# Three edits in the second mixer of a transformer kernel: the query rotation on VectorE, attention steps inside weight chunks, output turns and splits moved

## The chip, the cores and the metric

The kernel runs on one core of a Trainium2 chip. The metric is the time of one launch on the device in microseconds (us), lower is better. TensorE multiplies, VectorE (DVE in the rows), ScalarE (ACT) and GpSimd (POOL) do the elementwise work, and SyncE (SP) issues the loads.

## The reference

The reference is a small network on 256 tokens of width 1024 in float32: a mixer of gated recurrence, a product-key feed-forward of 16384 experts, a second mixer of two kinds of attention, a second such feed-forward, and one more block. The change lies in the second mixer:

```python
def mla_moba_mixer(x, positions, norm_mix, w_in, cq_norm, ckv_norm, w_uq, w_ukv,
                   mla_q_norm, mla_k_norm, moba_q_norm, moba_k_norm, w_out):
    xn = rmsnorm(x, norm_mix)
    c_q, c_kv, k_pe, q_d, k_d, v_d = split_cols(xn @ w_in, [Q_LORA, KV_LORA, C_ROPE, D_W, D_W, D_W])
    q_c = (rmsnorm(c_q, cq_norm) @ w_uq).reshape(B, S, C_HEADS, C_QK)
    ...
    q_c = rmsnorm(q_c, mla_q_norm)
    q_c = jnp.concatenate([q_c[..., :C_NOPE], rope(q_c[..., C_NOPE:], positions)], axis=-1)
    ...
    return jnp.concatenate([out_c, out_d], axis=-1) @ w_out
```

Here `rope` rotates the last 64 of a head's 192 columns, as two halves of 32, with a sine and a cosine for each position. There are four heads of the first attention (numbers 0 to 3 below) and four of the second (4 to 7).

## The kernel before

**Weights.** All large weights pass through one stream of 680 chunks of 128x1024 numbers (512 KB) in four slots. For chunk `i`, SyncE loads `raw` once the low part of chunk `i-4` is made (`load`), ScalarE copies it to `WH`, rounded, once chunk `i-4` has been used (`high`), and VectorE or GpSimd subtracts, which gives the remainder `WL` (`low_v`, `low_g`). TensorE then makes each product three times: high by high, high by low and low by high (`three`). So an engine's program is a written order of such steps with the side work between them, and each engine goes through its own order strictly. A step that waits holds all that stands behind it on its engine.

**Second mixer.** It takes chunks `L1` to `L1+23`. Chunks 0 to 15 (`l1_win`) give `z = xn @ w_in` in four blocks of four chunks, and chunks 16 to 23 (`l1_wout`) the output projection. The remainders of chunks 0, 1 and 2 are GpSimd's, those of 3 to 23 VectorE's, and those of the first chunks of the feed-forward behind it GpSimd's again. Chunks 0 and 1 are multiplied token tile by token tile (`nat_by_tile`): tile 0 of both, the turn (transposes through TensorE) of the normed tile 1, and then tile 1 of both. After a block's last chunk ScalarE copies token tile 0 of its result from PSUM into `Z`, and VectorE token tile 1 (in chunks 3, 7, 11 and 15, once the chunk is used).

**Side work.** `side(c)` runs after chunk `c` on each engine. VectorE scales queries and keys in `side(9)`. GpSimd makes the eight small trigonometric tables `TRG` (line 1973), rotates the shared key part (lines 1982 to 1985, `KPE`) and rotates the queries (the same lines, 128x256 each time). TensorE turns queries and keys in `side(10)` and `side(11)` (`turn_heads`, line 1520; `qr` are the rotated query parts). Attention is a pipeline of ten steps, `att_tensor(0)` to `att_tensor(9)`: step `i` makes the scores of head `i` (line 1552), turns the weights of head `i-1` (line 1559) and weighs the values of head `i-2` (lines 1570 to 1572). `att_vector` and `att_scalar` of the same number follow it, and so does the copy of a head's output to `O`. Steps 0 to 3 stand after chunks 12 to 15, steps 4 to 9 among chunks 16 to 21. `turn_o(kp)` turns the outputs of heads `2kp` and `2kp+1` (line 1580), and `split_o_scalar` and `split_o_vector` (lines 1732 and 1736) make high and low parts of them for chunks `16+2kp` and `17+2kp`. `last_out` multiplies chunks 22 and 23.

**Loads for the tables.** SyncE issues, after the last low part of the feed-forward in front (`g_low`), eight small loads on one semaphore, `tables1_in`: row gains, constants, `UQ`, `UKV` and four columns `GCOL` (line 1508). The table makers wait for all eight, which is 128. Only then does SyncE go on with the weights from chunk `L1+4`.

Of the kernel before, what the change touches and what calls it, by code (L numbers as in the profile page):

```python
# [7 lines left out]
ALU = mybir.AluOpType  # L8
# [29 lines left out]
L0, P0, L1, P1, B2, END = 0, 32, 304, 328, 600, 680  # L38
# [37 lines left out]
def build(nc, d, out):  # L76
    ctx = ExitStack()
    with ctx:
# [3 lines left out]
        def sem(name):  # L82
            return ctx.enter_context(nc.semaphore(name))
# [121 lines left out]
                              [v[:, k, :] for v in rows], k == 0, k == nk - 1)  # L205
            m.then_inc(w_used, 1)

        def chunk_nat(t, i, outs, kq, n, bank_free):

            wait_low(t, i)  # L210
            for tt in range(2):
                if kq == 0:
                    bank_free(tt)
                for kk in range(2):
                    k = kq * 2 + kk
                    if n is not None:
                        rows_in(t, n, tt, k)
                    m = three(t, outs[tt], [v[:, k, tt * 128:tt * 128 + 128] for v in (XH, XL)],
                              [v[:, i % NW, kk * 512:kk * 512 + 512] for v in (WH, WL)], k == 0, k == 7)
            m.then_inc(w_used, 1)  # L220

        def nat_by_tile(t, i, n, xs):
# [13 lines left out]
                if tt == 0:  # L236
                    turn(t, n, 1, xs)

        def chunk_out(t, i, kp, nb, first, bank_free):

            wait_low(t, i)
            for tt in range(2):
                if first:
                    bank_free(2 * nb + tt)
                for kk in range(2):
                    k = 2 * kp + kk
                    m = three(t, PS[:, 2 * nb + tt, :], [v[:, k, tt * 128:tt * 128 + 128] for v in (XH, XL)],
                              [v[:, i % NW, kk * 512:kk * 512 + 512] for v in (WH, WL)], first and kk == 0, False)
            m.then_inc(w_used, 1)

        def last_out(t, i, kps, ready, n, xs):
# [1180 lines left out]

        def peer_gpsimd(g, l):
            wq, down, up = bases(l)
            for c in range(272):
                low_g(g, wq + c + 2)


        Z = ar(0, 2, 2048)
# [25 lines left out]
            "lora_products", "qkv_by_scalar", "qkv_by_vector"))  # L1465


        squares, hq_ss, hq_sd, scaled, rotated = (sem(n) for n in (
            "heads_squares", "heads_sum", "qk_root", "qk_scaled", "rotated"))
        mo_sd, mo_up, hT, hT_a, hT_v = (sem(n) for n in (  # L1470
            "moba_root", "moba_scaled", "heads_turned", "heads_by_scalar", "heads_by_vector"))
        at_mm, at_mx, at_e, at_T, pt_a, pt_v, at_w, o_a, o_v = (sem(n) for n in (
# [111 lines left out]
        def mixer1_tensor(t):  # L1584
            def nat_bank(nb, tt):
                if nb >= 2:
                    t.wait_ge(z_v if tt else z_a, nb - 1)

            def side(c):
# [35 lines left out]
                if c == 11:  # L1625
                    t.wait_ge(hT_a, 1)
                    t.wait_ge(hT_v, 1)
                    t.wait_ge(scaled, 3)
                    turn_heads(t, "kr")
                    t.wait_ge(hT_a, 2)  # L1630
                    t.wait_ge(hT_v, 2)
                    t.wait_ge(rotated, 2)
                    turn_heads(t, "qr")
                if c >= 12:
                    att_tensor(t, c - 12)
                if c == 13:
                    t.wait_ge(mo_up, 1)
                    t.wait_ge(z_a, 3)
# [9 lines left out]
            for c in range(2, 16):  # L1648
                nb, kq = divmod(c, 4)
                chunk_nat(t, L1 + c, [PS[:, 2 * (nb % 2) + tt, :] for tt in range(2)], kq, 2 if nb == 0 else None,  # L1650
                          lambda tt: nat_bank(nb, tt))
                side(c)
            turn_o(t, 0)
            att_tensor(t, 4)
            for n in range(6):
                kp, nb = divmod(n, 2)
                if nb == 0 and kp > 0:
                    turn_o(t, kp)
                if n in (2, 4):
                    att_tensor(t, 4 + n)  # L1660
                t.wait_ge(o_l, kp + 5)
                chunk_out(t, L1 + 16 + n, kp, nb, kp == 0,
                          lambda b: t.wait_ge(z_v if b % 2 else z_a, 3 + b // 2))
                if n == 0:
                    att_tensor(t, 5)
                if n in (2, 4):
                    att_tensor(t, 5 + n)
            turn_o(t, 3)
            last_out(t, L1 + 22, (3,), lambda kp: t.wait_ge(o_l, 8), 3, XS)


# [67 lines left out]
        def mixer1_scalar(a):  # L1739
# [69 lines left out]
            high(a, L1 + 19)  # L1809
            att_scalar(a, 5)  # L1810
            high(a, L1 + 20)
            high(a, L1 + 21)
            split_o_scalar(a, 1)
            att_scalar(a, 6)
            high(a, L1 + 22)
            att_scalar(a, 7)
            high(a, L1 + 23)
            split_o_scalar(a, 2)
            att_scalar(a, 8)
            high(a, L1 + 24)  # L1820
            att_scalar(a, 9)
            table(a, ACT.Sqrt)
            high(a, L1 + 25)
            split_o_scalar(a, 3)


        def by_head(ss, n):
# [47 lines left out]
        def mixer1_vector(v):  # L1875
            norm_vector(v, 2, XS, PV_MIX1, lambda t, h: add_up(v, 1, t, h, P0 + 271, 2), True)

            def side(c):
# [31 lines left out]
                if c == 9:  # L1910
                    v.wait_ge(hq_sd, 1)
                    v.reciprocal(SM[:, 64:80], SM[:, 64:80]).then_inc(vec.sem, vec.up())
                    v.wait_ge(vec.sem, vec.n)
                    v.tensor_tensor(kc4[:, :, :, 0:128], kv4[:, :, :, 0:128], by_head(SSQK[:, :, 1, :], 128),
                                    ALU.mult).then_inc(scaled, 1)
                    v.tensor_tensor(q8, q8, by_head(SSQK[:, :, 0, :], 192), ALU.mult).then_inc(scaled, 1)
                    v.wait_ge(rotated, 1)
                    v.tensor_tensor(kc4[:, :, :, 128:192], KPE.unsqueeze(2).to_broadcast([128, 2, 4, 64]),
                                    by_head(SSQK[:, :, 1, :], 64), ALU.mult).then_inc(scaled, 1)
                if c == 10:  # L1920
                    turned_vector(v, "kn")
                    turned_vector(v, "qn")
# [25 lines left out]
            low_v(v, L1 + 18)  # L1948
            att_vector(v, 5)
            low_v(v, L1 + 19)  # L1950
            low_v(v, L1 + 20)
            split_o_vector(v, 1)
            att_vector(v, 6)
            low_v(v, L1 + 21)
            att_vector(v, 7)
            low_v(v, L1 + 22)
            split_o_vector(v, 2)
            att_vector(v, 8)
            low_v(v, L1 + 23)
            att_vector(v, 9)  # L1960
            low_v(v, L1 + 24)
            split_o_vector(v, 3)
            low_v(v, L1 + 25)

        def mixer1_gpsimd(g):
            si, co = TRIG[:, 0], TRIG[:, 1]
            low_g(g, L1 + 2)
            g.wait_ge(trig_up, 2)
            g.wait_ge(tables1_in, 128)
            for n in range(2):  # L1970
                g1, g2 = (GN[:, 192 * n + lo:192 * n + lo + 32].unsqueeze(1).to_broadcast([128, 2, 32]) for lo in (128, 160))
                for i, (a_, b_) in enumerate(((co, g1), (si, g2), (co, g2), (si, g1))):
                    g.tensor_tensor(TRG[n][:, i], a_, b_, ALU.mult).then_inc(gps.sem, gps.up())

            def rotate(x1, x2, o1, o2, tables, shape, last):
                n = 64 * (shape[2] if len(shape) == 4 else 1)
                t1, t2, t3, t4 = (ROT[:, i * n:i * n + n].rearrange(
                    "p (t h c) -> p t h c" if len(shape) == 4 else "p (t c) -> p t c", t=2, c=32) for i in range(4))
                g.wait_ge(gps.sem, gps.n)
                for o, a_, b_ in ((t1, x1, 0), (t2, x2, 1), (t3, x2, 2), (t4, x1, 3)):  # L1980
                    b_ = tables[:, b_].unsqueeze(2).to_broadcast(shape) if len(shape) == 4 else tables[:, b_]
                    g.tensor_tensor(o, a_, b_, ALU.mult).then_inc(gps.sem, gps.up())
                g.wait_ge(gps.sem, gps.n)
                g.tensor_tensor(o1, t1, t2, ALU.subtract).then_inc(gps.sem, gps.up())
                g.tensor_tensor(o2, t3, t4, ALU.add).then_inc(last, 1)

            g.wait_ge(z_a, 1)
            g.wait_ge(z_v, 1)
            rotate(Z[:, :, 384:416], Z[:, :, 416:448], KPE[:, :, 0:32], KPE[:, :, 32:64], TRG[1], [128, 2, 32], rotated)
            for t in range(2):  # L1990
                g.wait_ge(qkv_a, 2 * t + 1)
                g.wait_ge(qkv_v, 2 * t + 1)
                g.tensor_tensor(SQS[:, t], QC[:, t], QC[:, t], ALU.mult).then_inc(squares, 1)
            g.wait_ge(scaled, 2)
            x1, x2 = q8[:, :, :, 128:160], q8[:, :, :, 160:192]
            rotate(x1, x2, x1, x2, TRG[0], [128, 2, 4, 32], rotated)
            g.wait_ge(hq_ss, 2)
            g.wait_ge(z_a, 3)
            g.wait_ge(z_v, 3)
            w = Z[:, :, 1024:1536]  # L2000
            g.tensor_tensor(SQS[:, :, 0:512], w, w, ALU.mult).then_inc(squares, 1)
            for c in range(1, 24):
                low_g(g, L1 + c + 2)
# [596 lines left out]
```

## Time and profile before

| | |
|---|---|
| median of three runs | 2155.51 us (2153.27 to 2156.95) |
| the profiled execution's own time | 2158.37 us |
| its span | 2156.4 us |
| TensorE busy | 2113.5 us (98%) |
| VectorE busy | 1466.3 us (68%) |
| ScalarE busy | 1279.6 us (59%) |
| GpSimd busy | 374.3 us (17%) |
| granted TensorE clock, mean | 0.997 of full speed |
| second mixer in the span | about 938 to 1053 us |

A profile is one execution. Times in the rows are from the start of its span. The ends of products on TensorE are modelled and overlap the next ones, so their starts are the firmer figure: a product with 512 columns starts every 0.23 us though its row says 0.39.

### The profile page before, as it was taken

Reading aid. Unit: us, or ns where it says so; the run is one execution under the profiler, and the core shown is the slowest. Engines: PE = TensorE matmul, PEld = TensorE weight load, DVE = VectorE, ACT = ScalarE, POOL = GpSimd, SP = SyncE. Lnnn points to the kernel's source line nnn. Section 1 sums busy time; section 2 is a strip of 40 time slices with the busy share of each in tenths; the row PEclk is TensorE's granted clock in tenths of the full one; section 3 lists DMA queues with packets and bytes.
Section 4 is the critical chain, followed back from the end, with each engine's and each line's share of the span. In section 5 each row is a group of like instructions: output and inputs, shape, how many; then the busy total and the mean of one; then the engine's idle time right before and its main releaser. Section 6 shows DMA issues by size and latency. Waiting matters only on the chain.

```text
span 2156.4 us, 32225 instructions
## 1 busy us (share of the span) xinstructions
PE 2113.5 (98%) x12416; PEld 1828.2 (85%) x12416; DVE 1466.3 (68%) x2588; ACT 1279.6 (59%) x2177; POOL 374.3 (17%) x175
## 2 busy tenths in 40 slices
PE   8899999999999999999999999999999999999998
PEld 7779988888888888877799888888888888788997
DVE  7658988889855555557489888898555555433446
ACT  6665488877644444455545888776444444444464
POOL 1437800000000000031378000000000000253131
PEclk9999999999999999999999999999999999999999
DMA  6445655555566666653456555555666666754244
GB/s 221 141 143 164 183 174 167 165 176 166 160 203 194 195 195 194 193 183 111 122 164 185 172 166 170 172 170 158 205 194 194 194 193 193 262 182 156 79 137 127
DMA packets 105179, 373.16 MB, mean 173 GB/s; under 512 B 12172, under 2 KB 15652, under 8 KB 104644
## 3 DMA queue, kind: packets, MB, share of 16 engines
q1 hardware_dynamic: 105028, 371.11, 56.4%
q8 instruction: 99, 1.62, 0.3%
q14 instruction: 52, 0.43, 0.1%
HBM read 369.97 MB, written 1.10 MB: 172 GB/s over the span
## 4 chain that ended last, share of the span: by engine, by line
PE 91%; DVE 4%; ACT 3%; issue 1%; DMA 1%; POOL 1%; SPq 0%; DVEq 0%; ACTq 0%; POOLq 0%
PE ps L186 22%; PE ps L180 17%; PE ps L182 16%; PE ps L181 16%; PE ps L187 11%; PE ps L1008 3%; PE ps L2100 1%; PE ps L2078 1%; DVE WL L168 1%; PE ps L987 1%; DMA raw<-in_w_qk_dram 1%; PE ps L2086 1%; PE ps L1552 0%; ACT arena L287 0%; ACT WH L163 0%
## 5 line engine op out<-in xcount | busy, mean ns | idle before, releaser
L163 ACT ACTIVATE WH<-raw 128x1024 fp32r<-128x1024 f32 x680 | 717.1, 1056 | 466.4 <-PE ps L182 406.9
L186 PE MATMUL ps<-X,WH 128*128 128x512 f32 x2048 | 727.2, 399 | 0.7 <-DVE WL L168 0.6
L168 DVE TENSOR_TENSOR WL<-raw,WH 128x1024 fp32r<-128x1024 f32 x552 | 676.2, 1227 | 72.2 <-ACT WH L163 72.0
L173 POOL TENSOR_TENSOR WL<-raw,WH 128x1024 fp32r<-128x1024 f32 x128 | 321.1, 2513 | 1663.1 <-ACT WH L163 1662.3
L187 PE MATMUL ps<-X,WL 128*128 128x256 f32 x2048 | 571.3, 279 | 0.0
L186 PEld LDWEIGHTS ps<-X,WH 128*128 128x128 f32 x2048 | 384.4, 188 | 89.4 <-DVE WL L168 1.0
L180 PE MATMUL ps<-WH,X 128*128 128x512 f32 x960 | 379.2, 395 | 7.6 <-DVE X L1736 3.4
L187 PEld LDWEIGHTS ps<-X,WL 128*128 128x128 f32 x2048 | 386.0, 188 | 0.1
L182 PE MATMUL ps<-WH,X 128*128 128x512 f32 x960 | 374.9, 390 | 0.0
L181 PE MATMUL ps<-WL,X 128*128 128x512 f32 x960 | 374.9, 390 | 0.0
L180 PEld LDWEIGHTS ps<-WH,X 128*128 128x128 f32 x960 | 181.0, 188 | 49.0 <-DVE X L1736 4.1
L182 PEld LDWEIGHTS ps<-WH,X 128*128 128x128 f32 x960 | 180.9, 188 | 38.2
L181 PEld LDWEIGHTS ps<-WL,X 128*128 128x128 f32 x960 | 181.1, 189 | 37.0 <-issue 0.5
L180 PE MATMUL ps<-X,WH 128*128 128x256 f32 x704 | 201.4, 286 | 0.7 <-DVE WL L168 0.7
L181 PE MATMUL ps<-X,WH 128*128 128x256 f32 x704 | 199.2, 283 | 0.0
L182 PE MATMUL ps<-X,WL 128*128 128x256 f32 x704 | 199.2, 283 | 0.0
L1385 DVE TENSOR_TENSOR X<-arena,X 128x512 fp32r<-128x512 f32 x84 | 58.1, 692 | 161.9 <-ACT X L1172 161.9
L1125 ACT ACTIVATE ONE<-ONE,GATE 128x128 f16<-128x128 f16 x512 | 167.4, 429 | 0.0
L180 PE MATMUL ps<-WH,GH 128*128 128x512 f32 x352 | 137.3, 390 | 2.7 <-DVE GL L1385 2.7
L180 PEld LDWEIGHTS ps<-X,WH 128*128 128x128 f32 x704 | 134.9, 192 | 5.6 <-issue 2.7
L182 PE MATMUL ps<-WH,GL 128*128 128x512 f32 x352 | 137.0, 389 | 0.0
L181 PE MATMUL ps<-WL,GH 128*128 128x512 f32 x352 | 137.0, 389 | 0.0
(306 smaller groups left out, 2375.9 us busy)
## 6 DMA issues: line engine op xcount, KB each, us to landing
raw<-in_l_down_dram SPq DMA_DIRECT2D x256, 512.0 KB, 3.7
raw<-in_l_up_dram SPq DMA_DIRECT2D x256, 512.0 KB, 4.2
raw<-in_l_wq_dram SPq DMA_DIRECT2D x32, 512.0 KB, 3.6
raw<-in_w_qk_dram SPq DMA_DIRECT2D x24, 512.0 KB, 3.8
raw<-in_w_gates_dram SPq DMA_DIRECT2D x24, 512.0 KB, 3.6
raw<-in_l_nat_dram SPq DMA_DIRECT2D x16, 512.0 KB, 3.5
raw<-in_l_wout_dram SPq DMA_DIRECT2D x16, 512.0 KB, 3.7
raw<-in_l_win_dram SPq DMA_DIRECT2D x16, 512.0 KB, 3.7
```

Of the source, the lines that this page charges most:

```text
L163: a.activation(WH[:, i % NW, :], raw[:, i % NW, :], ACT.Copy).then_inc(w_high, 1)
L168: v.tensor_tensor(WL[:, i % NW, :], raw[:, i % NW, :], WH[:, i % NW, :], ALU.subtract).then_inc(w_low_v, 1)
L173: g.tensor_tensor(WL[:, i % NW, :], raw[:, i % NW, :], WH[:, i % NW, :], ALU.subtract).then_inc(w_low_g, 1)
L180: t.matmul(o, a[0], b[0], start=first, stop=False)
L181: t.matmul(o, a[0], b[1], start=False, stop=False)
L182: return t.matmul(o, a[1], b[0], start=False, stop=last)
L186: t.matmul(PS[:, bank, :], w[0], X2[:, k, :, :].rearrange("p w t -> p (w t)"), start=first, stop=False)
L187: return t.matmul(PS[:, bank, 0:256], w[1], X2[:, k, 0, :], start=False, stop=last)
L987: m = t.matmul(PS[:, 4 + h % 4, (2 * tt + q) * 128:(2 * tt + q) * 128 + 128], QT[:, j, tt * 128:tt * 128 + 128], KEYS[:, j * 128:j * 128 + ...
L1008: m = t.matmul(PS[:, 6 + j // 4, (j % 4) * 128:(j % 4) * 128 + 128], ONE[:, s % 2, 0, g, :, tt], ROWS[:, s % 2, 1 + k, g, :, tt], start=(k ...
L1125: a.activation(ROWS[:, s % 2, 1, g, :, t], ROWS[:, s % 2, 2, g, :, t], ACT.Copy, scale=GATE0[:, 8 * s + j:8 * s + j + 1]).then_inc(row_0, 1)
L1385: v.tensor_tensor(gl, G[:, 2 * p:2 * p + 2, :].rearrange("p e t -> p (e t)"), gh, ALU.subtract).then_inc(g_low, 1)
```

## The change

GpSimd makes the tables first of all, before the remainders of chunks 0, 1 and 2, the first two of which move there from the end of the feed-forward's loop. VectorE rotates the queries in `side(9)`. Steps 1 to 3 of the attention on TensorE move from behind chunks 13 to 15 to inside them: after three, two and one of the chunk's four groups of three products. `turn_o(1)` to `turn_o(3)` move from behind chunks 17, 19 and 21 to the middle of them. ScalarE and VectorE split these outputs ahead of the weight copies that stood in front. Of the order on VectorE and ScalarE in chunks 13 to 15 nothing is changed.

```diff
-        def chunk_nat(t, i, outs, kq, n, bank_free):
+        def chunk_nat(t, i, outs, kq, n, bank_free, amid={}):
...
+                    if 2 * tt + kk + 1 in amid:
+                        amid[2 * tt + kk + 1]()
...
-        def chunk_out(t, i, kp, nb, first, bank_free):
+        def chunk_out(t, i, kp, nb, first, bank_free, amid=None):
...
+                if tt == 0 and amid:
+                    amid()
...
         def peer_gpsimd(g, l):
             wq, down, up = bases(l)
-            for c in range(272):
+            for c in range(270 if l == 0 else 272):
                 low_g(g, wq + c + 2)
...
-                    t.wait_ge(rotated, 2)
+                    t.wait_ge(rotated, 3)
                     turn_heads(t, "qr")
-                if c >= 12:
-                    att_tensor(t, c - 12)
+                if c == 12:
+                    att_tensor(t, 0)
...
                 chunk_nat(t, L1 + c, [PS[:, 2 * (nb % 2) + tt, :] for tt in range(2)], kq, 2 if nb == 0 else None,
-                          lambda tt: nat_bank(nb, tt))
+                          lambda tt: nat_bank(nb, tt), {16 - c: lambda: att_tensor(t, c - 12)} if c >= 13 else {})
                 side(c)
             turn_o(t, 0)
             att_tensor(t, 4)
             for n in range(6):
                 kp, nb = divmod(n, 2)
-                if nb == 0 and kp > 0:
-                    turn_o(t, kp)
-                if n in (2, 4):
-                    att_tensor(t, 4 + n)
                 t.wait_ge(o_l, kp + 5)
                 chunk_out(t, L1 + 16 + n, kp, nb, kp == 0,
-                          lambda b: t.wait_ge(z_v if b % 2 else z_a, 3 + b // 2))
-                if n == 0:
-                    att_tensor(t, 5)
-                if n in (2, 4):
-                    att_tensor(t, 5 + n)
-            turn_o(t, 3)
+                          lambda b: t.wait_ge(z_v if b % 2 else z_a, 3 + b // 2),
+                          (lambda: turn_o(t, kp + 1)) if nb else None)
+                if n < 5:
+                    att_tensor(t, n + 5)
             last_out(t, L1 + 22, (3,), lambda kp: t.wait_ge(o_l, 8), 3, XS)
...
             high(a, L1 + 20)
+            split_o_scalar(a, 1)
             high(a, L1 + 21)
-            split_o_scalar(a, 1)
             att_scalar(a, 6)
             high(a, L1 + 22)
             att_scalar(a, 7)
+            split_o_scalar(a, 2)
             high(a, L1 + 23)
-            split_o_scalar(a, 2)
             att_scalar(a, 8)
             high(a, L1 + 24)
             att_scalar(a, 9)
+            split_o_scalar(a, 3)
             table(a, ACT.Sqrt)
             high(a, L1 + 25)
-            split_o_scalar(a, 3)
...
+                    x1, x2 = q8[:, :, :, 128:160], q8[:, :, :, 160:192]
...
+                    v.wait_ge(tables_up, 8)
+                    v.wait_ge(scaled, 2)
+                    for o, x, i in ((t1, x1, 0), (t2, x2, 1), (t3, x2, 2), (t4, x1, 3)):
+                        v.tensor_tensor(o, x, TRG[0][:, i].unsqueeze(2).to_broadcast([128, 2, 4, 32]),
+                                        ALU.mult).then_inc(vec.sem, vec.up())
+                    v.wait_ge(vec.sem, vec.n)
+                    v.tensor_tensor(x1, t1, t2, ALU.subtract).then_inc(rotated, 1)
+                    v.tensor_tensor(x2, t3, t4, ALU.add).then_inc(rotated, 1)
...
         def mixer1_gpsimd(g):
             si, co = TRIG[:, 0], TRIG[:, 1]
-            low_g(g, L1 + 2)
             g.wait_ge(trig_up, 2)
             g.wait_ge(tables1_in, 128)
             for n in range(2):
...
-                    g.tensor_tensor(TRG[n][:, i], a_, b_, ALU.mult).then_inc(gps.sem, gps.up())
...
+                    g.tensor_tensor(TRG[n][:, i], a_, b_, ALU.mult).then_inc(tables_up, 1)
+            for c in range(3):
+                low_g(g, L1 + c)
...
-            g.wait_ge(scaled, 2)
-            x1, x2 = q8[:, :, :, 128:160], q8[:, :, :, 160:192]
-            rotate(x1, x2, x1, x2, TRG[0], [128, 2, 4, 32], rotated)
```

`split_o_vector(v, 1)`, `(v, 2)` and `(v, 3)` move on VectorE in the same way: the first ahead of `low_v(L1+20)`, the second ahead of `low_v(L1+22)`, the third stays behind `att_vector(v, 9)`. The calls `low_v(L1+24)` and `low_v(L1+25)`, which did nothing because these remainders are GpSimd's, are gone.

## Rows read from the trace of the kernel before

**Rows 1.** The page: the chain of work that ended last, by engine.

```profile
PE 91%; DVE 4%; ACT 3%; issue 1%; DMA 1%; POOL 1%; SPq 0%; DVEq 0%; ACTq 0%; POOLq 0%
```

**Rows 2.** TensorE's waits over the whole span: releaser, us in total, times, longest.

```profile
PE ps L180 <- DVE X L1736: 3.4, 3, 2.0
PE ps L1580 <- ACT arena L1727: 2.1, 1, 2.1
```

**Rows 3.** GpSimd's timeline, 934 to 951 us: start, us, engine, line, form, idle before.

```profile
934.47 4.75 POOL L173 TENSOR_TENSOR WL<-raw,WH 128x1024 fp32r<-128x1024 f32 x2 [666.99 <-ACT WH L163]
942.18 2.37 POOL L173 TENSOR_TENSOR WL<-raw,WH 128x1024 fp32r<-128x1024 f32 x1 [2.97 <-ACT WH L163]
944.51 5.27 POOL L1973 TENSOR_TENSOR arena<-trig,arena 128x64 f32<-128x64 f32 x8
```

**Rows 4.** The tile GCOL: its four loads, durations and starts, and time to landing.

```profile
L1508 SPq DMA_DIRECT2D gcol<-in_rows_dram x4: 427/479/542, 933.0 to 934.6; - x4
...
DMA to landing us min/median/max: 4.4/4.7/5.1
```

**Rows 5.** Line 1973, the tables: ns shortest, median and longest of eight.

```profile
L1973 POOL TENSOR_TENSOR arena<-trig,arena x8: 322/332/1313, 944.5 to 948.5; 128x64 f32<-128x64 f32 x8
```

**Rows 6.** TensorE's and VectorE's timelines at the mixer's start.

```profile
938.17 0.39 PE L180 MATMUL ps<-WH,X 128*128 128x512 f32 x1
...
942.20 1.09 PE L397 MATMUL ps<-cst,arena 128*128 128x128 f32 x8 [1.15 <-DVE arena L344]
943.74 0.50 PE L180 MATMUL ps<-WH,X 128*128 128x512 f32 x1 [0.45 <-DVE X L350]
...
945.84 3.76 DVE L168 TENSOR_TENSOR WL<-raw,WH 128x1024 fp32r<-128x1024 f32 x3 [0.34 <-ACT WH L163]
```

**Rows 7.** VectorE's timeline, 981 to 985 us.

```profile
981.62 0.68 DVE L1918 TENSOR_TENSOR arena<-arena,sm 128x512 f32<-128x512 f32 x1
982.22 1.75 DVE L168 TENSOR_TENSOR WL<-raw,WH 128x1024 fp32r<-128x1024 f32 x1
983.89 1.40 DVE L1690 TENSOR_SCALAR arena<-ps,gcol 128x512 f32<-128x512 f32 x2
```

**Rows 8.** TensorE's timeline: the turn of the rotated queries, and chunk 12.

```profile
988.64 1.03 PE L1520 MATMUL ps<-cst,arena 128*64 128x128 f32 x8 [1.89 <-POOL arena L1985]
989.43 0.48 PE L180 MATMUL ps<-WH,X 128*128 128x512 f32 x1
```

**Rows 9.** VectorE's, ScalarE's and TensorE's timelines behind chunk 15.

```profile
1009.98 0.69 DVE L1944 COPY arena<-ps 128x512 f32<-128x512 f32 x1 [0.58 <-PE ps L182]
1011.87 0.56 DVE L1852 SCALAR_TENSOR_TENSOR arena<-ps,arena 128x384 f32<-128x384 f32 x1 [1.20 <-PE ps L1552]
...
1013.11 0.40 ACT L1712 ACTIVATE arena<-arena,sm 128x128 f32<-128x128 f32 x1 [2.53 <-DVE sm L1856]
...
1015.13 0.63 PE L1580 MATMUL ps<-cst,arena 128*128 128x128 f32 x4 [2.15 <-ACT arena L1727]
```

**Rows 10.** ScalarE's and TensorE's timelines among chunks 17 to 22.

```profile
1023.37 0.61 ACT L1727 ACTIVATE arena<-ps,sm 128x128 f32<-128x128 f32 x2
...
1024.41 0.60 PE L1580 MATMUL ps<-cst,arena 128*128 128x128 f32 x4
...
1027.14 0.50 PE L180 MATMUL ps<-WH,X 128*128 128x512 f32 x1 [0.47 <-DVE X L1736]
...
1045.89 0.50 PE L180 MATMUL ps<-WH,X 128*128 128x512 f32 x1 [1.98 <-DVE X L1736]
```

**Rows 11.** Windows: TensorE busy, weight loads, DVE, ACT, POOL, granted clock, DMA share, GB/s.

```profile
84.00:87.00 3.00, 0.00 (x0) 0.00 (x0) 1.99 (x2) 2.98 (x3) 3.00 (x2) 1.00 0.49 175
88.00:91.00 3.00, 3.00 (x12) 2.52 (x12) 1.82 (x2) 1.04 (x2) 1.72 (x1) 0.53 0.26 96
...
1047.40:1050.70 3.30, 3.30 (x9) 2.58 (x8) 1.15 (x2) 0.72 (x2) 0.00 (x0) 0.50 0.56 159
```

More of the change, by code:

```diff
@@ L1465, in build @@
             "lora_products", "qkv_by_scalar", "qkv_by_vector"))
-        squares, hq_ss, hq_sd, scaled, rotated = (sem(n) for n in (
-            "heads_squares", "heads_sum", "qk_root", "qk_scaled", "rotated"))
+        squares, hq_ss, hq_sd, scaled, rotated, tables_up = (sem(n) for n in (
+            "heads_squares", "heads_sum", "qk_root", "qk_scaled", "rotated", "trig_gained"))
         mo_sd, mo_up, hT, hT_a, hT_v = (sem(n) for n in (
@@ L1919, in side @@
                                     by_head(SSQK[:, :, 1, :], 64), ALU.mult).then_inc(scaled, 1)
+                    x1, x2 = q8[:, :, :, 128:160], q8[:, :, :, 160:192]
+                    t1, t2, t3, t4 = (ROT[:, i * 256:i * 256 + 256].rearrange("p (t h c) -> p t h c", t=2, c=32)
+                                      for i in range(4))
+                    v.wait_ge(tables_up, 8)
[6 more added lines that the diff above has]
+                    v.tensor_tensor(x2, t3, t4, ALU.add).then_inc(rotated, 1)
                 if c == 10:
@@ L1950, in mixer1_vector @@
             low_v(v, L1 + 19)
+            split_o_vector(v, 1)
             low_v(v, L1 + 20)
-            split_o_vector(v, 1)
             att_vector(v, 6)
@@ L1955, in mixer1_vector @@
             att_vector(v, 7)
+            split_o_vector(v, 2)
             low_v(v, L1 + 22)
-            split_o_vector(v, 2)
             att_vector(v, 8)
@@ L1960, in mixer1_vector @@
             att_vector(v, 9)
-            low_v(v, L1 + 24)
             split_o_vector(v, 3)
-            low_v(v, L1 + 25)
         def mixer1_gpsimd(g):
             si, co = TRIG[:, 0], TRIG[:, 1]
-            low_g(g, L1 + 2)
             g.wait_ge(trig_up, 2)
@@ L1972, in mixer1_gpsimd @@
                 for i, (a_, b_) in enumerate(((co, g1), (si, g2), (co, g2), (si, g1))):
-                    g.tensor_tensor(TRG[n][:, i], a_, b_, ALU.mult).then_inc(gps.sem, gps.up())
[L1975 to L1985, printed above, removed]
+                    g.tensor_tensor(TRG[n][:, i], a_, b_, ALU.mult).then_inc(tables_up, 1)
+            for c in range(3):
+                low_g(g, L1 + c)
+            x1, x2, o1, o2 = Z[:, :, 384:416], Z[:, :, 416:448], KPE[:, :, 0:32], KPE[:, :, 32:64]
+            t1, t2, t3, t4 = (ROT[:, i * 64:i * 64 + 64].rearrange("p (t c) -> p t c", t=2) for i in range(4))
+            g.wait_ge(tables_up, 8)
             g.wait_ge(z_a, 1)
             g.wait_ge(z_v, 1)
-            rotate(Z[:, :, 384:416], Z[:, :, 416:448], KPE[:, :, 0:32], KPE[:, :, 32:64], TRG[1], [128, 2, 32], rotated)
+            for o, x, i in ((t1, x1, 0), (t2, x2, 1), (t3, x2, 2), (t4, x1, 3)):
+                g.tensor_tensor(o, x, TRG[1][:, i], ALU.mult).then_inc(gps.sem, gps.up())
+            g.wait_ge(gps.sem, gps.n)
+            g.tensor_tensor(o1, t1, t2, ALU.subtract).then_inc(gps.sem, gps.up())
+            g.tensor_tensor(o2, t3, t4, ALU.add).then_inc(rotated, 1)
             for t in range(2):
```

## The prediction, made before the change was run

> **What bounds the kernel now.** I read the page first. The chain that ended last is TensorE's for 91% of the span [rows 1], so only what moves TensorE's products counts, and all that lies behind the second mixer shifts with them. Then I read TensorE's own waits, because a stall of the bounding engine is the only thing that such a change can remove. In this mixer they are few: 2.1 us before the first turn of outputs and 3.4 us in three waits for split outputs [rows 2], and 1.9 us before the turn of the rotated queries [rows 8]. The last of the three costs more than it shows, for behind it the clock fell [rows 11]. Third came the timelines of all engines around every moved step. The reader should see there who is in front of the step on its own engine.
>
> **The tables go first: a loss at the start.** GpSimd now makes eight tables before the remainder of chunk 0, and they wait for eight loads. The last of these is issued at 934.6 and lands no earlier than 4.4 us later, at 939.0 (5.1 us: 939.7) [rows 4]. Before, GpSimd had chunk 0's remainder under way at 934.47 [rows 3], and TensorE's first products of the mixer stood at 938.17 [rows 6].
>
> How long do the tables take? They took 5.27 us [rows 3], yet the shortest of them 0.322, the median 0.332 and the longest 1.313 [rows 5]. The long ones lie where VectorE makes three remainders, 945.84 to 949.6 [rows 6]. In the new place VectorE makes none, for its first remainder comes after tile 1's rows. I take 8 x 0.33 = 2.6 us; the bound is 5.3. The Trainium skill's GPSIMD Engine Reference (Specifications) says that GpSimd shares its SBUF interfaces with VectorE and contends with its instructions of two SBUF inputs. The trace agrees (0.33 beside 1.31), and by that rule the sum has the short price.
>
> So tables end at 941.7. A remainder takes 4.75/2 = 2.37 us [rows 3], so those of chunks 0, 1 and 2 end at 944.0, 946.4 and 948.8. Chunk 0's six products on tile 0 start at 944.1, and chunk 1's at 946.5. Twelve products took from 938.17 to the last start at 942.20 - 1.15 - 0.39 = 940.66, so 0.227 us each [rows 6], and six take 1.4: 947.9. From the turn to tile 1's first product are 943.74 - 942.20 = 1.54 us [rows 6]. Tile 1 starts at 949.4 in place of 943.74: **5.7 us late at full clock.** TensorE idles from 938.2 to 944.1, 5.9 us. After an idle stretch that holds 84 to 87 us the granted clock was 0.53 in 88 to 91 [rows 11], so I expect half speed here. At 0.45 us each chunk 1's six products take 2.7, and tile 1 starts at 950.7: 7.0 us late. I take **+6.5**, ends +5.7 and +9.3 (tables at 5.3 us). Nothing absorbs it: loads of chunks 4 to 6 are issued behind these remainders, but chunk 4 is needed 8 us after tile 1 starts and a load takes some 4, and its two copies 2.3.
>
> **Queries rotated by VectorE.** The rotation's six operations are 128x256. VectorE shows 128x512 at 982.22 - 981.62 = 0.60 us from start to start [rows 7]. I take 0.33 (bounds 0.30, by elements alone, and 0.60), so with the wait between the four and the two 2.1 us (1.8 to 3.6), and nothing else hides it. Behind it on VectorE stand chunk 12's remainder (982.22 before, now 984.3; 1.2 us, a third of 3.76 [rows 6]) and the two copies of 0.7 us that took place at 983.89 [rows 7]. They end at 986.8, where TensorE's turn of the rotated queries needs them. That turn could start at 986.9 or after the turn in front of it: chunk 11 ends at 988.64 - 1.89 - 1.03 = 985.7 [rows 8], the turn of the rotated keys must wait for the first copy until 986.2 and takes 0.8. So chunk 12 starts at 987.8 and not at 989.43 [rows 8]: **-1.6**. No later weight is then late; VectorE has over 1 us of slack before chunks 13 and 14.
>
> **Steps 1 to 3 inside chunks 13 to 15: what VectorE does first decides.** TensorE does the same work in another order. Before, chunk 15 ended at 1009.8 and step 3 at 1012.8; now both are done at 1011.2, with the 1.6 us. The aim would be that step 3's chain runs under the chunk's last nine products. But in VectorE's order the copy of `Z` stands ahead of `att_vector(3)`, and it waits until chunk 15 is used. So the chain starts only at the chunk's end: 0.2 us to the copy and 0.6 for it, then 1013.11 - 1011.87 = 1.24 to ScalarE's exponentials, then 1015.13 - 1013.11 = 2.02 to the turn [rows 9]. 1011.2 + 4.1 = 1015.3, against 1015.13. **+0.1, and the 1.6 us before it are given back: +1.7.** TensorE idles 4.1 us there instead of 2.15. Near enough to the idle stretch in [rows 11] that I expect half clock behind it: 3.3 us at 0.50 lose 1.65, **+1.6** (0 if not).
>
> **Turns in mid-chunk, splits ahead of copies.** `turn_o(1)` needs head 3's output, whose copies end at 1023.98, and TensorE turns it at 1024.41 [rows 10]. In the middle of chunk 17, six products earlier, at 1023.0, it must wait till 1024.1. Then come the turn, six products (1.4) and step 6, which with the turn take 1027.14 - 0.5 - 0.2 - 1024.41 = 2.0: chunk 18 starts at 1027.5, against 1027.14 [rows 10]. The wait of 0.5 is gone and one of 1.1 is there. The same holds for `turn_o(2)`, where one of about 1.0 goes; both together cost 0.3. `turn_o(3)` is different: its head 7 is ready in time, half a chunk covers the splits of 0.6 and 0.7 us, and ScalarE's table load and chunk copy no longer stand ahead. The wait of 1.98 [rows 10] goes with 0.2 around it. Together **-1.9** (-1.4 to -2.0).
>
> **The clock behind `last_out`.** Behind that wait the clock was 0.50 for 1047.40 to 1050.70 [rows 11]; without the wait I expect full clock, **-1.6** (0 if it falls anyway). The Trainium skill's TensorE: Matmul & The Clock Gate (What's actually happening) says that the slow clock is the default and activity lifts it. By that rule, with which the trace agrees, the first two idle stretches cost and this one is won.
>
> **Sum.** +6.5 - 1.6 + 1.7 + 1.6 - 1.9 - 1.6 = +4.7 us on the profiled execution's 2158.4 (span 2156.4 and 2 us around it): 2163.1. The median of the runs is 2155.5, 2.9 below, so the forecast is 2155.5 + 4.7 = **2160.2 us**.
>
> **Rivals.**
> - *The clock does not fall* behind the two new idle stretches. For it: how long a fall lasts and when it begins is seen in two places only. Then 5.7 + 0.1 - 1.9 - 1.6 = +2.3: 2157.8 us.
> - *Step 3 does run under chunk 15.* VectorE's order speaks against it. The turn would come at 1011.5, 3.6 us early, without idling: 6.5 - 3.6 - 1.9 - 1.6 = -0.6: 2154.9 us.
> - *The other side, faster:* the table loads don't hold chunk 0. It decides whether all eight have landed by 934.47 - 2.6 = 931.9, or the tables are otherwise hidden. Then 0.1 - 1.9 - 1.6 = -3.4: 2152.1, and a little more with a better clock. Against it: the last load is issued at 934.6.
> - *Everything at its upper end:* tables at 5.3 us, half clock at all three places: 9.3 + 0.1 + 1.6 - 1.4 = +9.6: 2165.1 us.
>
> **How the numbers follow.** A measurement of this kernel tells about 0.2% (4.3 us) from no change. Chances: forecast 0.46 and upper end 0.08, both slower: 0.54. Clock rival 0.28 and step 3 rival 0.08: within 0.2%: 0.36. The other side 0.10, which I count as faster. The range goes from 2156.5, a little under the clock rival for the spread of medians, to 2165.0; it leaves out the step 3 rival and the faster one, 0.18.
>
> **What would show it.** On GpSimd the eight tables at 939 to 941.7 and then three remainders up to 948.8; TensorE's first product of the mixer at 944 and a wait for line 173, which the trace before hardly has; tile 1 near 950. Chunk 12 then starts 1.6 us earlier in relation to tile 1. VectorE's copy of line 1944 (its line after) ahead of step 3 with TensorE waiting 4 us before the first turn. Waits of about 1 us inside chunks 17 and 19, none before `last_out`. Granted clock of about 0.5 at the mixer's start and behind the first turn, 1.00 in `last_out`. I would be wrong if the tables start before 939, if the rotation on VectorE costs over 3 us, or if the clock stays up.

## The result, and the profile after

The changed kernel is slower: median 2164.33 us (2161.41 to 2165.19, six runs) against 2156.23 us (2153.27 to 2158.36, six runs) before. The ratio is 1.0037, with an interval of 1.0026 to 1.0048, or +8.1 us: small, but clear of the noise. The profiled execution took 2164.03 us (span 2162.1). The forecast was +4.7 us.

This page's chain by engine answers to [rows 1]: TensorE is still what sets the end.

```profile
PE 92%; DVE 3%; ACT 2%; issue 1%; POOL 1%; DMA 0%; SPq 0%; DVEq 0%; ACTq 0%; POOLq 0%
```

TensorE's waits, as [rows 2] (releaser, us in total, times, longest). The three waits for split outputs are gone. There is a new one of 7.5 us for GpSimd, and that for ScalarE grew from 2.1 to 3.9, with two more behind it:

```profile
PE ps L180 <- POOL WL L173: 7.5, 1, 7.5
PE ps L1585 <- ACT arena L1726: 5.7, 3, 3.9
```

The mixer's start, on SyncE, GpSimd and TensorE (start, us, engine, line, form, idle before and its releaser); these answer to [rows 3, 4, 6]:

```profile
928.55 2.46 SPq L1510 DMA_DIRECT2D arena<-in_l_uq_dram  x1
```

```profile
L1513 SPq DMA_DIRECT2D gcol<-in_rows_dram x4: 428/431/878, 931.5 to 933.4; - x4
...
DMA to landing us min/median/max: 3.9/4.6/4.8
```

```profile
938.35 2.71 POOL L1981 TENSOR_TENSOR arena<-trig,arena 128x64 f32<-128x64 f32 x8 [670.82 <-DMA gcol<-in_rows_dram]
941.01 7.00 POOL L173 TENSOR_TENSOR WL<-raw,WH 128x1024 fp32r<-128x1024 f32 x3
```

```profile
932.09 1.09 PE L402 MATMUL ps<-cst,arena 128*128 128x128 f32 x8 [0.19 <-DVE arena L349]
943.41 0.79 PE L180 MATMUL ps<-WH,X 128*128 128x512 f32 x1 [7.48 <-POOL WL L173]
...
950.30 0.50 PE L180 MATMUL ps<-WH,X 128*128 128x512 f32 x1 [0.45 <-DVE X L355]
```

This profile reached the mixer 2.4 us sooner than that of before (932.09 for the turn of tile 0 against 934.48), in code that nothing changed. The lead grows evenly through the first feed-forward. It isn't laid to the change: of two profiles of one and the same kernel, that with the short idle products below, one has it (931.52) and one hasn't (934.41). So each stage is measured from a mark inside the mixer. Three intervals carry the reading: from the turn of tile 0 to tile 1's first product (the start), from there to `turn_o(0)`, and from the turn of tile 0 to the first product of line 186 in the feed-forward behind the mixer (the stage).

| us | start | to `turn_o(0)` | stage |
|---|---|---|---|
| before | 9.26 | 71.39 | 130.69 |
| after | 18.21 | 71.74 | 138.43 |

The stage is 7.7 us longer, nearly the loss by the medians (8.1). The two profiled executions differ by 5.7, since one came to the stage sooner. The start alone lost 8.95; all behind it together won 1.2.

VectorE's timeline and TensorE's, as [rows 7, 8]: six rotations, then the remainder, and TensorE turns keys and queries in one go, with no wait for GpSimd.

```profile
988.76 1.42 DVE L1926 TENSOR_TENSOR arena<-arena 128x256 f32<-128x256 f32 x4
990.22 0.43 DVE L1929 TENSOR_TENSOR arena<-arena 128x256 f32<-128x256 f32 x1
990.56 0.42 DVE L1930 TENSOR_TENSOR arena<-arena 128x256 f32<-128x256 f32 x1
990.90 1.22 DVE L168 TENSOR_TENSOR WL<-raw,WH 128x1024 fp32r<-128x1024 f32 x1
```

```profile
992.88 1.91 PE L1525 MATMUL ps<-cst,arena 128*64 128x128 f32 x16 [0.46 <-issue]
994.54 0.47 PE L180 MATMUL ps<-WH,X 128*128 128x512 f32 x1
```

VectorE, ScalarE and TensorE behind chunk 15, as [rows 9]. The copy of `Z` still stands ahead of step 3, and TensorE, which was done with step 3 long before, waits 3.89 us:

```profile
1018.18 0.69 DVE L1955 COPY arena<-ps 128x512 f32<-128x512 f32 x1 [3.93 <-PE ps L182]
1018.79 0.55 DVE L1851 SCALAR_TENSOR_TENSOR arena<-ps,arena 128x384 f32<-128x384 f32 x1
```

```profile
1020.02 0.40 ACT L1711 ACTIVATE arena<-arena,sm 128x128 f32<-128x128 f32 x1 [1.24 <-DVE sm L1855]
```

```profile
1022.04 1.08 PE L1585 MATMUL ps<-cst,arena 128*128 128x128 f32 x4 [3.89 <-ACT arena L1726]
...
1033.60 0.63 PE L1585 MATMUL ps<-cst,arena 128*128 128x128 f32 x4 [0.92 <-ACT arena L1726]
...
1043.98 0.63 PE L1585 MATMUL ps<-cst,arena 128*128 128x128 f32 x4 [0.91 <-ACT arena L1726]
...
1053.63 0.50 PE L180 MATMUL ps<-WH,X 128*128 128x512 f32 x1
```

The lower three answer to [rows 10]: two waits of 0.9 inside chunks 17 and 19, and none before `last_out`.

Windows, columns as in [rows 11], with the window's length as the first figure; the granted clock comes before the DMA share. In the upper two it is half speed, each behind a long wait. In `last_out`, where before showed 0.50, it is 1.00:

```profile
940.00:948.00 8.00, 4.59 (x11) 3.60 (x12) 0.00 (x0) 0.00 (x0) 8.00 (x7) 0.50 0.35 105
...
1022.00:1026.00 4.00, 3.96 (x18) 3.70 (x18) 2.18 (x5) 0.92 (x3) 0.00 (x0) 0.50 0.01 4
...
1053.00:1057.00 4.00, 3.97 (x18) 2.96 (x17) 1.57 (x3) 3.03 (x5) 1.97 (x2) 1.00 0.40 131
```

### The profile page after: what moved, and what is told of

Read it like the earlier page. It is cut to its first block, busy times and chain, and to the rows that moved or that the text cites. A ratio compares the mean times of both kernels' runs of the same rounds, so it can differ in the third digit from the quotient of the medians.

```text
span 2162.1 us, 32225 instructions
## 1 busy us (share of the span) xinstructions
PE 2114.4 (98%) x12416; PEld 1831.3 (85%) x12416; DVE 1467.4 (68%) x2594; ACT 1280.2 (59%) x2177; POOL 364.9 (17%) x169
## 4 chain that ended last, share of the span: by engine, by line
PE 92%; DVE 3%; ACT 2%; issue 1%; POOL 1%; DMA 0%; SPq 0%; DVEq 0%; ACTq 0%; POOLq 0%
PE ps L186 22%; PE ps L180 17%; PE ps L182 17%; PE ps L181 17%; PE ps L187 11%; PE ps L1013 3%; PE ps L2102 1%; PE ps L2080 1%; DVE WL L168 1%; PE ps L992 1%; PE ps L1557 1%; PE ps L2088 1%; ACT arena L292 0%; DVE X L355 0%; PE ps L1035 0%
```

## The experiments

All medians stand beside that of before on the same chip. "Stage" and "start" are the intervals of the table above, in the one profile of each kernel. A profile that holds one more stretch of slow clock than another is some 1.7 us longer for it (`last_out` took 7.65 us with one and 6.02 without), so small differences between stages are no firmer than those between medians.

| kernel | median | before | ratio, interval | start | to `turn_o(0)` | stage |
|---|---|---|---|---|---|---|
| remainders first | 2154.69 | 2156.31 | 0.9994, 0.9985 to 1.0003 | 9.25 | 71.77 | 128.55 |
| + step 3 ahead of `Z` | 2149.62 | 2156.31 | 0.9969, 0.9958 to 0.9979 | 9.25 | 69.55 | 125.69 |
| + turns behind 17, 19 | 2150.31 | 2156.88 | 0.9965, 0.9951 to 0.9979 | 9.25 | 67.90 | 122.80 |
| tables first alone | 2164.24 | 2156.31 | 1.0038, 1.0024 to 1.0052 | 16.46 | 71.40 | 137.09 |
| turns and splits alone | 2155.38 | 2156.31 | 0.9993, 0.9984 to 1.0002 | 9.27 | 71.41 | 129.20 |
| rotation alone | 2154.02 | 2155.23 | 0.9991, 0.9982 to 0.9999 | 9.26 | 69.94 | 128.33 |
| steps inside alone | 2157.89 | 2155.23 | 1.0011, 1.0002 to 1.0019 | 9.26 | 73.14 | 131.68 |
| gains on their own semaphore | 2157.06 | 2155.23 | 1.0003, 0.9994 to 1.0012 | 10.90 | 71.75 | 131.32 |
| clock held, long | 2168.37 | 2155.23 | 1.0053, 1.0040 to 1.0066 | 21.31 | 74.41 | 141.63 |
| clock held, short | 2164.91 | 2156.88 | 1.0042, 1.0029 to 1.0056 | 16.06 | 71.77 | 133.74 |
| clock held, short, again | 2162.45 | 2154.82 | 1.0035, 1.0024 to 1.0046 | 15.90 | 71.74 | 133.61 |
| the change again | 2162.86 | 2154.82 | 1.0038, 1.0024 to 1.0052 | 17.33 | 71.74 | 137.55 |

**Undoing one part: the remainders of chunks 0 to 2 stand ahead of the tables again.**

```diff
         def mixer1_gpsimd(g):
             si, co = TRIG[:, 0], TRIG[:, 1]
+            for c in range(3):
+                low_g(g, L1 + c)
             g.wait_ge(trig_up, 2)
...
-            for c in range(3):
-                low_g(g, L1 + c)
```

> The changed kernel, but GpSimd makes the remainders of chunks 0, 1 and 2 before the tables, as before the change. Theory (the tables' loads hold the first chunk): in the changed trace the mixer's tile 1 stood 9.0 us late, so this kernel is 7 to 9 us faster than the changed one, 2155.5 to 2157.5 us, level with the kernel before within 2 us; TensorE's wait of 7.5 us for line 173 is gone and the granted clock stays at 1.00 at the mixer's start, while the wait of 3.9 us before the first turn and the clock of 0.5 behind it remain. Rival (the loss lies in the steps inside chunks): the time stays within 2 us of 2164, and the stall moves behind chunk 2.

Measured: 2154.69 us, 9.6 less than the whole change. The start is 9.25, as before. On GpSimd:

```profile
935.73 4.74 POOL L173 TENSOR_TENSOR WL<-raw,WH 128x1024 fp32r<-128x1024 f32 x2 [667.33 <-ACT WH L163]
...
945.77 5.26 POOL L1983 TENSOR_TENSOR arena<-trig,arena 128x64 f32<-128x64 f32 x8
```

The tables take 5.26 us here, beside VectorE's remainders, and 2.71 in the changed kernel's place, where VectorE had only two short operations. In this place nothing waits for them: the short tables were bought with TensorE's idling. The order on GpSimd, together with the wait for the loads that stands in it, is the loss.

**The other half of step 3: on VectorE and ScalarE it goes ahead of chunk 15's `Z` copy too** (on top of the last kernel; ScalarE in the same way).

```diff
             for c in range(16):
                 low_v(v, L1 + c + 2)
+                if c == 15:
+                    att_vector(v, 3)
                 if c % 4 == 3:
...
-                if c >= 12:
+                if 12 <= c < 15:
                     att_vector(v, c - 12)
```

> As e1_remainders_first, and in chunk 15 VectorE and ScalarE do step 3 of the attention ahead of their copies of Z. Theory (the copy of Z, which waits for the whole chunk, gives back what steps inside chunks gain): the wait before the first turn falls from 3.9 us to under 0.6 us, the clock stays at 1.00 behind it, and the time falls by 3.6 us for the chain and 2.5 us for the clock against e1, to about 2150 us, faster than the kernel before by 0.25%. Rival (the chain from scores to the output is the limit anyway): under 1 us of gain.

Measured: 2149.62 us, faster than before by 0.31%. VectorE's and TensorE's timelines:

```profile
1009.86 0.56 DVE L1853 SCALAR_TENSOR_TENSOR arena<-ps,arena 128x384 f32<-128x384 f32 x1 [0.70 <-PE ps L1557]
...
1013.09 0.69 DVE L1959 COPY arena<-ps 128x512 f32<-128x512 f32 x1 [1.96 <-PE ps L182]
```

```profile
1013.12 0.63 PE L1585 MATMUL ps<-cst,arena 128*128 128x128 f32 x4
```

Step 3 runs under the chunk's last products, and the first turn follows them with no wait. The stage is only 2.9 us shorter than the last kernel's: this profile, the slowest of its eight executions (2152.79), has slow clock at 943 to 948 (0.66) and at 1053 to 1057 (0.57), where the other has none. It was VectorE's and ScalarE's order that kept TensorE's new place for the step from being worth anything.

**The tables first, alone, on the kernel before.**

```diff
-            for c in range(272):
+            for c in range(270 if l == 0 else 272):
...
         def mixer1_gpsimd(g):
             si, co = TRIG[:, 0], TRIG[:, 1]
-            low_g(g, L1 + 2)
             g.wait_ge(trig_up, 2)
...
+            for c in range(3):
+                low_g(g, L1 + c)
```

> The kernel before with one edit: GpSimd makes the tables before the remainders of chunks 0, 1 and 2. Theory: the same loss as in the changed kernel, tile 1 of the mixer 7 to 9 us late with half clock for chunk 1's products, 2163 to 2165 us. Rival: the loss needs the other edits; then under 2 us.

Measured: +7.9 us, as much as the whole change, and TensorE's wait is there:

```profile
PE ps L180 <- POOL WL L173: 7.0, 1, 7.0
```

**The turns and splits alone** (`turn_o(1)` to `turn_o(3)` in mid-chunk, splits ahead of the weight copies; on the kernel before).

> The kernel before with only the outputs' turns in mid-chunk and the splits ahead of the weight copies. Theory: the waits of 0.5, 1.0 and 2.0 us before chunks 18, 20 and 22 become two of about 1 us inside chunks 17 and 19, which gives 1.7 to 1.9 us, and the clock stays up in the last chunks, which gives 1.6 us: 2152.7 us, 0.15% faster than before. Rival: the gain is lost inside the chunks, and the time is that of before within 1 us.

Measured: -0.9 us, not -2.8; the stage is 1.5 shorter. The waits are as forecast (0.92 and 0.91 inside, none before `last_out`), and the clock did stay up at 1047 to 1051. But it fell behind the wait of 2.15 us before the first turn, which is in the kernel before as well [rows 9] and had no fall behind it there (1.00 at 1015 to 1022):

```profile
1016.00:1020.00 4.00, 4.00 (x19) 3.63 (x18) 2.54 (x7) 1.53 (x6) 0.00 (x0) 0.57 0.01 4
...
1047.00:1051.00 4.00, 4.00 (x19) 3.30 (x18) 1.57 (x4) 2.58 (x6) 2.40 (x1) 1.00 0.44 131
```

So the waits' own time is won (3.43 us of them became 1.83), and the slow clock was as long in this profile as before. That the fall moved because a wait was removed isn't shown: the next kernel removes neither wait and shows the same.

**The rotation alone** (on VectorE, the rest as in the kernel before).

> The kernel before with only the rotation of the queries on VectorE (tables made behind the three remainders, attention steps, turns and splits as before). Theory: chunk 12 starts 1.4 to 1.6 us earlier, and as step 3 stands behind chunk 15 and the copy of Z is not in its way, all of it reaches the end: about 1.5 us faster than before, 2154.7 us. Rival: the rotation on VectorE (2.1 us) delays copies and remainders so much that nothing is gained.

Measured: -1.2 us by the medians, and the way from tile 1 to `turn_o(0)` is 1.45 shorter. TensorE's waits of 2.15 us before `turn_o(0)` (1013.86) and of 1.98 us before `last_out` (1046.10) are both there, as before. The windows behind them:

```profile
1013.00:1017.00 4.00, 3.14 (x13) 2.88 (x14) 1.35 (x3) 1.31 (x4) 0.00 (x0) 0.57 0.00 0
1046.00:1050.00 4.00, 3.90 (x17) 3.24 (x18) 1.48 (x4) 0.83 (x3) 1.28 (x1) 1.00 0.58 168
```

The clock fell behind the first and not behind the second; in the profile of before it was the other way round. The kernel with the tables first alone has the same two waits and shows the same as this one (0.59 at 1021 to 1025, 1.00 at 1053 to 1057).

**Steps 1 to 3 inside chunks 13 to 15, alone.**

> The kernel before with only steps 1 to 3 of the attention inside chunks 13 to 15. Theory: the copy of Z stands ahead of step 3 on VectorE, so the first turn comes 1.8 to 2.0 us later than before, TensorE idles about 4 us there and the clock halves behind it for another 1.6 to 2.5 us: 2159 to 2161 us. Rival: the steps overlap as they are meant to and the kernel is 2 us faster.

Measured: +2.7 us; the way to `turn_o(0)` is 1.75 longer, and the wait before the turn is 3.9 in place of 2.15. Behind it the clock is slow at 1017 to 1021 (0.57). But the stage is only 1.0 longer, since the two slow stretches that before has behind it are missing (1.00 at 1049.5 to 1053.5 behind the wait of 1.98); so where the rest of the 2.7 comes from isn't shown. Together with the rotation that is -1.45 + 1.75 = +0.30, and the whole change showed 71.74 - 71.39 = +0.35.

The four parts add up by their medians to 7.9 - 0.9 - 1.2 + 2.7 = +8.5, against +8.1 for all of them. That is no proof that they don't bear on each other: each of the four has an interval of about 2 to 3 us to either side. By the stages they add up to 6.4 - 1.5 - 2.4 + 1.0 = +3.5, against +7.7 (+6.9 in the second profile of the change). A part of that gap is the slow stretches, which lie at other places in each profile.

**Only the load that the tables read.** The tables stay first, but wait for the load of the row gains alone, the first of the eight.

```diff
-            s.dma_start(GN, d["rows"][0:1, RW_MQ:RW_MQ + 640].to_broadcast([128, 640])).then_inc(tables1_in, 16)
+            s.dma_start(GN, d["rows"][0:1, RW_MQ:RW_MQ + 640].to_broadcast([128, 640])).then_inc(gains_in, 16)
...
-            g.wait_ge(tables1_in, 128)
+            g.wait_ge(gains_in, 16)
             for n in range(2):
```

> The changed kernel, but the load of the row gains, the only one of the eight that the tables read, has a semaphore of its own, and the tables wait for it alone. Theory (the landing of the last of eight loads sets the start): the tables start about 6 us earlier, chunk 0's remainder is ready 1 to 2 us after TensorE wants it, and the kernel is 6 to 8 us faster than the changed one, 2156 to 2158 us. Rival (GpSimd's own work of 2.7 us for the tables is the loss): under 3 us of gain.

Measured: +1.8 us against before, not clear of the noise, and 6.3 less than the change (each against its own before). GpSimd:

```profile
933.07 2.28 POOL L1981 TENSOR_TENSOR arena<-trig,arena 128x64 f32<-128x64 f32 x8 [665.47 <-DMA arena<-in_rows_dram]
935.31 7.51 POOL L173 TENSOR_TENSOR WL<-raw,WH 128x1024 fp32r<-128x1024 f32 x3
```

The tables start 5.3 us earlier. TensorE's waits for the remainders shrink from 7.48 to 1.73 and 0.70, and there is no slow clock behind them. So of the start's loss of 8.95 us, 7.3 went with the wait for seven loads that the tables don't read, the slow clock behind it included. The rest, 1.6, is what the tables' own time still costs.

**The clock held up.** The idle stretches are filled with products that compute nothing (identity by identity, into a part of PSUM that is overwritten afterwards), 60 ahead of the mixer's first chunk and 30 ahead of `turn_o(0)`. The two waits ahead of the 30 are for the copies of turned heads out of that part of PSUM, not for what `turn_o(0)` waits for.

```diff
+            idle_products(t, 0, 60)
             nat_by_tile(t, L1, 2, XS)
...
+            t.wait_ge(hT_a, 6)
+            t.wait_ge(hT_v, 6)
+            idle_products(t, 0, 30)
             turn_o(t, 0)
```

> The changed kernel with idle products on TensorE in its two long waits: 60 in front of the mixer's first chunk and 30 in front of the first turn of outputs, all into a bank that is overwritten afterwards; they add no result. Theory (the clock's fall costs 1.6 us at the start and 2.5 us behind the turn): granted clock of 1.00 at both places, and about 4 us faster than the changed kernel, 2160 us. Rival: the fall costs nothing because the work behind it waits for other engines; then within 1 us of 2164, or slower if the products outlast the waits.

Measured: +13.1 us. Each such product took 0.22 us, so 60 took 13.3 and outlasted the wait. The clock did stay up:

```profile
936.00:948.00 12.00, 12.00 (x102) 11.71 (x101) 3.94 (x12) 3.60 (x10) 8.41 (x11) 1.00 0.29 103
```

Shortened to 32 and 16:

> As e7_clock_held_up, whose idle products took 0.22 us each and outlasted both waits, with 32 and 16 of them (7.1 and 3.6 us, against waits of 7.5 and 3.9 us). Theory (behind both waits half clock costs time in the changed kernel): granted clock of 1.00 at both places, tile 1 of the mixer 16.6 us behind the turn of tile 0 instead of 18.2, the first turn to the second 9.3 us instead of 11.6, and 3 to 4 us faster than the changed kernel, 2160.5 us. Rival: the clock's part is made up elsewhere; within 1 us of 2164.

Measured: +8.0 us, although the stage is 4.7 shorter than the change's. So it was run again, with the change itself beside it:

> The kernel of e9_clock_held_short again. Its profiled stage was 4.7 us shorter than the changed kernel's, its median not. Theory (the fall of the clock costs about 4 us, and the earlier median was hidden by waits elsewhere): 3 to 5 us faster than e11. Rival (what the held clock gives in the stage is lost elsewhere in the program, as a wait for a weight at the third block's start was seen): within 1.5 us of e11, the stage again shorter, and the time before and behind it again longer.

> The changed kernel itself, run beside the next one on one chip. Both theories: about 2164 us. It is the reference for the clock's price, because the earlier comparison crossed chips and calls.

Measured: 2162.45 against 2162.86, so 0.4 us for a stage 3.9 us shorter. The seven runs spread from 2159.83 to 2165.92, so a gain of 1 or 2 us could hide there; the two profiled executions differ by 1.7. Most of the time is given back at the third block's first weights. ScalarE's and TensorE's timelines there, first with the idle products, then the change as it is:

```profile
1870.87 1.06 ACT L163 ACTIVATE WH<-raw 128x1024 fp32r<-128x1024 f32 x1 [7.48 <-DMA raw<-in_w_qk_dram]
```

```profile
1873.24 0.50 PE L186 MATMUL ps<-X,WH 128*128 128x512 f32 x1 [3.23 <-DVE WL L168]
```

```profile
1872.66 1.06 ACT L163 ACTIVATE WH<-raw 128x1024 fp32r<-128x1024 f32 x1 [4.51 <-DMA raw<-in_w_qk_dram]
```

```profile
1875.03 0.50 PE L186 MATMUL ps<-X,WH 128*128 128x512 f32 x1 [0.25 <-DVE WL L168]
```

ScalarE waits for a load that lands late. The DMA share is about 1.05 in both just before, so this load may stand behind full queues. Take the time from SyncE's issue of the last small load but one ahead of it (line 2041, or 2045 with the idle products) to this copy. With the idle products it is 1870.87 - 1849.05 = 21.8 us, and without them 1872.66 - 1852.80 = 19.9. All three profiles with idle products show 21.1 to 22.1 there; the eleven others 19.9 to 20.2. So the late load goes with the idle products, though they stand 900 us ahead of it. Why is open.

**The turns behind their chunks again.** On the kernel with step 3 ahead, only `turn_o(3)` stays in mid-chunk.

```diff
-                          (lambda: turn_o(t, kp + 1)) if nb else None)
+                          (lambda: turn_o(t, kp + 1)) if n == 5 else None)
+                if n in (1, 3):
+                    turn_o(t, kp + 1)
```

> As e2_step3_ahead, but turn_o(1) and turn_o(2) stand behind chunks 17 and 19 again and only turn_o(3) stays in mid-chunk; splits stay ahead of the weight copies. Theory (in mid-chunk these two turns wait 0.9 us for heads 3 and 5, while behind the chunk nothing makes them wait and the splits are in time): both waits go, 1.8 us faster than e2, 2147.8 us. Rival (the turn inside gives as much as it costs, as the prediction had it within 0.3 us): within 0.5 us of e2.

Measured: 2150.31 us, ratio 0.9965, with 0.9969 for the kernel that it is built on; the intervals overlap. In the profile the waits inside chunks 17 and 19 (0.92 and 0.91) have given way to none behind chunk 17 and two of 0.26 and 0.41 behind chunk 19:

```profile
1030.74 0.63 PE L1585 MATMUL ps<-cst,arena 128*128 128x128 f32 x4 [0.26 <-ACT arena L1728]
1032.78 0.50 PE L180 MATMUL ps<-WH,X 128*128 128x512 f32 x1 [0.41 <-DVE X L1737]
```

That is 1.2 us less waiting. The stage is 2.9 shorter, but 1.7 of that is the slow clock at the start of the other kernel's profile, which no part of this edit touches. A faster median than the kernel with all turns inside isn't shown. Both beat the kernel before and the change.

## Why the prediction was nearly right, step by step

The direction, the place of the loss and the range (2156.5 to 2165.0) held, the range with 0.7 us to spare; the size came out 3.4 us short. By the profile the stage lost 7.7 where 4.7 were summed. The range also left out the forecast's own upper end (2165.1), so 0.26 of the chances lay outside it and not 0.18.

- **The start, +6.5: right in kind, too small; measured +8.95.** It was the largest miss, of 2.4 us. The tables' 2.6 us came out at 2.71. The first wrong term was the landing of the loads. The forecast had the tables start 939.0 - 934.48 = 4.5 us behind the turn of tile 0; they started 938.35 - 932.09 = 6.3 behind it. The last of the eight was issued 1.3 us behind that turn and not 0.1 (the issue of `UQ` took 2.46 us here; before, it took 0.43 and that of the constants 1.55), and the tables came 4.95 us after it, where the forecast took the shortest landing of [rows 4], 4.4. The long issue isn't the cause by itself: in the second profile of the change `UQ` took 0.43 and the last load was issued 0.4 us ahead of the turn, and yet the tables stood 5.4 behind the turn, 5.9 after that issue; the start was 17.33 there, +8.1. So the time until all eight had landed was taken too short, for both profiles. The second was the choice between clocks: I named 7.0 for half clock, expected half clock, and took 6.5. The granted clock was 0.50 from 940 to 948, and from the first product to tile 1 it took 6.89 us, where 6.6 belonged to half clock. The Trainium skill's GPSIMD Engine Reference (Specifications) says that GpSimd contends with VectorE's instructions of two SBUF inputs. The traces agree: 5.26 us for the tables beside VectorE's remainders, and 2.71 away from them.
- **The rotation, -1.6: right, -1.45.** Six operations took 990.90 - 988.76 = 2.14 us, forecast 2.1. Chunk 12 stands 994.54 - 950.30 = 44.24 behind tile 1; before it was 45.69.
- **Step 3, +0.1 net: right, +0.35.** VectorE's copy of `Z` decided, as argued from its order. The kernel that changes only that order won 5.1 us by the medians, more than the wait of 3.89.
- **Slow clock behind the first turn, +1.6: right in kind, too small.** From `turn_o(0)` to the end of chunk 16 the products took 2.5 us longer. The forecast counted 3.3 us of slow products; the window shows 4 us at 0.50, and more at its edges. But the whole 2.5 isn't the price of the longer wait: three other kernels fell to 0.57 to 0.59 behind the old wait of 2.15 us, which shows no fall in the one profile of before.
- **Turns and splits, -1.9: right.** `turn_o(0)` to `last_out` is 31.59 against 30.76; less the 2.5 of the clock that is -1.7. Both waits of 0.9 and the missing third stand in the rows.
- **Full clock in `last_out`, -1.6: right in this profile, and not because of the step named.** From the first product of `last_out` to the next turn it is 6.02 against 7.65, and behind it a second fall of before (the clock was 0.56 at 1057.2 to 1060.2) is missing too, -0.8, which I had not seen. The step "without the wait I expect full clock" held for the place. That it was a gain rests on the one profile of before: the tables first alone, the rotation alone and the steps inside alone all keep this wait of 1.98 us and show 1.00 behind it. So that -1.6 came true in these two profiles is luck in part. The turns and splits alone gave 0.9 us by the medians, where the two terms made 3.5.

The terms measured are 8.95 + 0.35 + 2.5 - 1.7 - 1.6 - 0.8 = +7.7. Of the rivals, "the clock does not fall" is out: it fell behind both waits in both profiles of the change. "Step 3 does run" and "the loads don't hold chunk 0" are out by the rows. What the upper end took for the start (+9.3) is nearly what came, though for another reason: late loads and not slow tables. What the slow clock costs the whole kernel isn't settled. Holding it up shortened the stage by 3.9 us and the median by 0.4, within a wide spread, and all three profiles with idle products have a late load of their own.

## What to carry to other kernels

Before a small preparation is put ahead of work that the bounding engine needs, read what it waits for. Here 2.7 us of tables hung on eight loads of which they read one, and that cost most of 8 us; in their old place they took twice as long and cost nothing. When a step is moved on one engine, look at the engines behind it in its chain too: on TensorE alone the move was a loss of 2.7 us, and with it in place, taking VectorE and ScalarE along won 5.1 us. (Both together against neither wasn't run; by the sum they win 2.4.) A term for the clock that rests on one profile should be taken with doubt: of two waits of about 2 us that three kernels share, the clock fell behind the second in the kernel before and behind the first in the two others. A second profile of the kernel before would have shown how firm such a term is.

## What the runs showed of the hardware that was not expected

- Behind waits of 3.9 us and more that were left idle, the granted clock fell to half in every profile. Behind the waits of about 2 us it was irregular: before, it fell at `last_out` (1.98 us) and not behind the first turn's 2.15 us; with the tables first alone, the rotation alone and the turns alone, it fell behind those 2.15 us, and in the first two not behind the 1.98. It also fell where no wait just before was over 1.2 us: at 1057 us before (0.56), at 943 (0.66) and 1053 us (0.57) with step 3 ahead.
- An identity product of 128x128 float32 numbers took 0.22 us as filler.
- Issue of small loads by SyncE took 0.43 us as a rule and 1.15 to 2.46 us for the constants' or `UQ`'s load in five profiles. Where neither was slow, one of the four `GCOL` loads took 0.86 to 1.34. By the start of the tables, the eighth landed 9.9 to 10.8 us behind the first issue in the six profiles that show the tables waiting for it.
- Idle products in one mixer went with a load 900 us later that landed 1 to 2 us later in relation to the loads issued before it, in three profiles of three.
